# Products of the identity with itself in TensorE's waits, in a kernel of two transformer blocks

## What is computed

```python
a = modulate(rmsnorm(h), shift, scale)
y = conformer_conv(a)     # layer 0: GLU, 31-tap depthwise conv, layernorm, silu, matmul
y = window_attention(a)   # layer 1: 16 heads, 4 kv heads, window 128, plus 256 context keys
h = h + g1 * y
h = h + g2 * conv_ffn(modulate(rmsnorm(h), ...))   # 1024 -> 2*2816, 3-tap conv, silu gate, -> 1024
```

## Time and profile before

| | |
|---|---|
| median of 3 runs | 2484.35 us |
| lowest and highest | 2482.55 and 2489.43 us |
| profiled execution, device time | 2481.34 us |
| profiled execution, span | 2479.5 us |
| mean granted clock over the span | 0.981 |
| TensorE busy | 2360.1 us, 95% |
| VectorE, ScalarE, GpSimd busy | 49%, 35%, 1% |
| moved by DMA | 387.5 MB |

### The profile page before, as it was taken

The page is one execution under the profiler, slowest core; times in us unless marked ns, Lnnn a source line. Parts: engine busy times, 40 slices in busy tenths (PEclk is TensorE's granted clock), DMA queues, the critical chain, the costliest instruction groups (busy, mean ns, idle before and its releaser), DMA issues. The chain is left out here.

```text
span 2479.5 us, 33877 instructions
## 1 busy us (share of the span) xinstructions
PE 2360.1 (95%) x13786; PEld 1808.2 (73%) x13786; DVE 1213.3 (49%) x1866; ACT 860.3 (35%) x1322; POOL 37.1 (1%) x57
## 2 busy tenths in 40 slices
PE   6999999999999999999899999999998889999997
PEld 4994779999999987677688888875897643333322
DVE  3898556552455342674664565754543422233224
ACT  4125553321233242583542344346444310101101
POOL 0000000000000001100000000000000100000000
PEclk8999999999999999999899999999999999999999
DMA  6248612121122142001232232210341669999996
GB/s 247 69 122 306 238 68 71 65 82 46 60 68 73 64 179 69 29 2 68 93 100 96 94 103 93 84 58 2 105 145 45 257 269 409 421 420 422 421 421 268
DMA packets 74242, 387.51 MB, mean 156 GB/s; under 512 B 8576, under 2 KB 12928, under 8 KB 43264
## 3 DMA queue, kind: packets, MB, share of 16 engines
q1 hardware_dynamic: 74112, 385.66, 41.2%
HBM read 380.22 MB, written 2.10 MB: 154 GB/s over the span
## 5 line engine op out<-in xcount | busy, mean ns | idle before, releaser
L314 PE MATMUL PS<-XNH,WHI 128*128 128x384 f32 (+2 forms) x1888 | 593.7, 358 | 16.4 <-issue 4.4
L269 DVE TENSOR_TENSOR WLO<-RAW,WHI 128x1024 fp32r<-128x1024 f32 (+3 forms) x226 | 279.1, 1235 | 645.8 <-ACT WHI L258 645.6
L314 PE MATMUL PS<-XNH,WLO 128*128 128x384 f32 (+2 forms) x1888 | 585.5, 354 | 0.0
L314 PE MATMUL PS<-XNL,WHI 128*128 128x384 f32 (+2 forms) x1888 | 585.1, 353 | 0.0
L258 ACT ACTIVATE WHI<-RAW 128x1024 fp32r<-128x1024 f32 (+3 forms) x226 | 241.5, 1068 | 772.8 <-PE PS L314 755.6
L314 PEld LDWEIGHTS PS<-XNH,WHI 128*128 128x128 f32 x1888 | 348.6, 189 | 52.5 <-issue 17.2
L314 PEld LDWEIGHTS PS<-XNL,WHI 128*128 128x128 f32 x1888 | 349.3, 189 | 32.1 <-issue 3.4
L314 PEld LDWEIGHTS PS<-XNH,WLO 128*128 128x128 f32 x1888 | 349.0, 189 | 29.5
L2994 PE MATMUL PS<-RAWM,XS 128*64 128x512 f32 x1024 | 237.5, 599 | 9.5 <-DMA RAWM<-experts 8.9
L2994 PEld LDWEIGHTS PS<-RAWM,XS 128*64 128x64 f32 x1024 | 68.1, 136 | 140.6 <-issue 104.8
L314 PE MATMUL PS<-HH,WHI 128*128 128x384 f32 (+1 forms) x528 | 158.0, 353 | 0.0
(11 more groups left out here) (358 smaller groups left out, 2560.3 us busy)
## 6 DMA issues: line engine op xcount, KB each, us to landing
RAWM<-experts SPq DMA_DIRECT2D x191, 1024.0 KB, 14.7
RAW<-up SPq DMA_DIRECT2D x88, 512.0 KB, 3.2
ADAW<-ada SPq DMA_DIRECT2D x26, 1024.0 KB, 7.4
RAW<-down SPq DMA_DIRECT2D x32, 704.0 KB, 4.0
ADAG<-ada SPq DMA_DIRECT2D x14, 1024.0 KB, 9.6
RAW<-pw SPq DMA_DIRECT2D x24, 512.0 KB, 3.5
ADAL<-ada SPq DMA_DIRECT2D x8, 1024.0 KB, 7.3
RAW<-qkv SPq DMA_DIRECT2D x12, 512.0 KB, 3.3
```

The costliest lines, as they stand in the source:

```text
L269: dve.tensor_tensor(prog.WLO[:, at % SPLITS, 0:to.length], prog.RAW[:, at % RAWS, 0:to.length], f32(prog.WHI[:, at % SPLITS, 0:to.length]) ...
L314: last = pe.matmul(prog.PS[:, to, at:at + b - a], w, x[:, k, a:b], start=(k == 0 and n == 0), stop=(k == g.k - 1 and n == 2))
```

## The change

A new helper issues n fp32 products of the identity with itself, 128 by 128 by 128, into 128 columns of a PSUM bank. Nothing reads them and no semaphore counts them. 180 of them are placed in TensorE's streams. Two waits are added, both on TensorE: in the attention ahead of the 8 products (both counts are waited for again by the first transposes), and at the end of `project`.

```diff
+def idle_products(prog, pe, bank, n):
+    to = prog.PS[:, bank // 2, bank % 2 * 512:bank % 2 * 512 + P]
+    for _ in range(n):
+        pe.matmul(to, prog.IDENT[:], prog.IDENT[:], start=True, stop=True)
...
 gated_convolution, tensor:
             for n in range(ADA_RING, KD):
                 first.multiply_slice(pe, n)
+            idle_products(prog, pe, 3, 5)
             first.turn_round(pe, 0)
+            idle_products(prog, pe, 3, 9)
...
 LayerNormSilu.on_tensor:
+        idle_products(self.prog, pe, 6, 3)
         pe.wait_ge(self.mean_kept, 1)
         spread_blocks(self.prog, pe, self.mean, ...)
+        idle_products(self.prog, pe, 6, 8)
         for k in range(KD):
+            if k >= 1:
+                idle_products(self.prog, pe, 6, 1)
             pe.wait_ge(self.squared, k + 1)
...
         for n in range(2):
             self.ada.multiply_slice(pe, n)
+        idle_products(self.prog, pe, 6, 5)
         pe.wait_ge(self.inverted, 1)
         spread_blocks(self.prog, pe, self.rstd, ...)
-        for n in range(2, 4):
-            self.ada.multiply_slice(pe, n)
+        self.ada.multiply_slice(pe, 2)
+        idle_products(self.prog, pe, 0, 6)
+        self.ada.multiply_slice(pe, 3)
+        idle_products(self.prog, pe, 0, 5)
...
 convolution_output, tensor:
             for n in range(6, KD):
                 ada.multiply_slice(pe, n)
+            idle_products(prog, pe, 6, 4)
             pe.wait_ge(ada.kept, 1)
...
             multiply_gap_slices(prog, pe, 0, range(GAP_FIRST))
+            idle_products(prog, pe, 2, 4)
...
 project, tensor:
             multiply_all(prog, pe, g, xh, xl, lambda u: segments, psum_free, None)
+            pe.wait_ge(psum_free, 4 + g.n - 3)
+            idle_products(prog, pe, 0, 5)
...
 conv_ffn, tensor (squares is None in ffn1):
             norm.sums_on_tensor(pe)
             if squares is not None:
                 multiply_gap_slices(prog, pe, 0, range(GAP_FIRST, GAP_SLICES))
+            else:
+                idle_products(prog, pe, 3, 6)
             norm.spread_on_tensor(pe)
             if squares is not None:
                 for n in range(GAP_SLICES, KD):
+                    idle_products(prog, pe, 3, 4)
                     ada.multiply_slice(pe, n)
+                idle_products(prog, pe, 3, 6)
+            else:
+                idle_products(prog, pe, 3, 14)
...
 window_qkv, tensor:
             for n in range(GAP_SLICES, KD):
+                idle_products(prog, pe, 3, 6)
                 ada.multiply_slice(pe, n)
...
 window_attention, rest_on_tensor:
         for n in range(1, BUFS):
             scores(pe, n)
+        pe.wait_ge(psum_free, kept(10))
+        pe.wait_ge(sined, 9)
+        idle_products(prog, pe, 5, 8)
         for n in range(STEPS):
...
         values(pe, STEPS - 1)
+        idle_products(prog, pe, 4, 5)
...
 latent_attention, tensor, at the end:
+            idle_products(prog, pe, 0, 7)
...
 memory_output, tensor:
             for n in range(2, len(blocks_of)):
                 turn(n)
+            idle_products(prog, pe, 1, 45)
             pe.wait_ge(slots, 1)
...
             last.then_inc(slot_turned, 1)
+            idle_products(prog, pe, 1, 4)
...
 experts, tensor:
+            idle_products(prog, pe, 1, 4)
             for k in range(KD):
                 gather(0, k)
```

## The result

| | before | after |
|---|---|---|
| median, first comparison (4 and 4 runs) | 2484.14 us | 2469.92 us, ratio 0.9949 [0.9929, 0.9969] |
| median, second comparison (17 and 7 runs) | 2480.84 us | 2469.99 us, ratio 0.9961 [0.9945, 0.9976] |
| profiled execution, device time and span | 2481.34, 2479.5 us | 2470.45, 2468.6 us |
| mean granted clock | 0.981 | 0.992 |
| TensorE busy | 2360.1 us | 2388.0 us |

The change makes the kernel faster by 14.2 us in the first comparison and 10.9 in the second. 2474.0 was forecast, with 2464 to 2482 as the range.

The account below looks back on a forecast made before the run. Experts' DMA bounds the end; ahead of it, blocks follow by barriers and low clock costs where TensorE is late. Terms sum to 9.1 us, 2481.3 to 2472.2; allowing for the higher median gives 2474.0, range 2464 to 2482.

Parts of the forecast that it names:

- The price of a product: All places: one identity product takes 0.24 us of TensorE at full clock and 0.44 at half clock.
- Do the products hold the clock: All places: the added products were expected to keep the clock at 1.00, as a dense run of this shape did.
- rival 2: Products don't hold the clock and run at half; the router's slot turn comes 6.5 us late; 2493.6 us, chance 0.05.
- Gain 2.3: `pw1`: 2.7 us from a full-clock first pair, less a net delay of 0.4; between -1.5 and 3.5.
- nothing is added between the DMA-bound slices: `pw1`: with no products among the slices, the clock falls at 36.29 as before, so five products take 2.2 us.
- ACT's squares are the bound and nothing is won: `pw2`: ACT is busy 3.41 of 3.41 us at 247.9, so no gain; 0.3 us lost over the groups.
- The slice lands at 349.23: `ffn0`: slice 7 and six products end at 351.5, first pair started at 351.66; gain 0.1 us, -0.3 to 1.5.
- a sign of being wrong: `ffn0` and `qkv`: first pairs starting over 0.5 us later than their slice allows would show the prediction wrong.
- The upper bound: `ffn1`: 3.3 us gained if the clock holds at its norm; 1.2 was taken, between -1.5 and 3.3.
- Rival 3: More is held than counted: `ffn1` in full 2.1, `ffn0`'s norm 1.5, low stretches' placement elsewhere 3; 2467 us, chance 0.09.
- Rival 4: Every low microsecond was a loss: TensorE late through all eight stretches, 28 us; 2456 us, chance 0.02.
- Rival 1: Too little is late on TensorE: only `wo`, `mem_in` and the gather gain, 4.6 less 1.2 us; 2481 us, chance 0.24.

Follow-up runs that it names:

- experiment 4: Changed kernel with all 180 products one column wide instead of 128: 2502.68 us, ratio 1.010 to the kernel before.
- experiment 1: Kernel before with only the 20 products at the attention's start and end and the end of `mla`: 2477.9 us against 2480.89, ratio 0.9989.
- experiment 2: Kernel before with only the 107 products in the norms, around the slices and at the end of `project`: 2475.1 us, ratio 0.9981.
- experiment 3: Kernel before with only the 53 products of the router and the gather: 2477.78 us, ratio 0.9990.
- experiment 7: Changed kernel with products also at still-low places, none before `pw1`'s turn round, slightly fewer at `ffn1`'s spread and the slots' wait: 2465.64 us, ratio 0.9935 to before.
- experiment 10: Kernel of experiment 7 without its 34 products inside `pw2`'s layernorm: 2464.49 us, ratio 0.9922 to the kernel before.
- experiment 9: Kernel of experiment 7 with five products ahead of each of `pw1`'s slices 4 to 7: 2464.62 us, ratio 0.9928 to the kernel before.
- experiment 11: Kernel of experiment 9 with two products, not four, ahead of `ffn0`'s slices 6 and 7, and two, not six, behind: 2461.58 us, ratio 0.9922 to before.
- experiment 12: Kernel of experiment 9 once more, unedited, beside experiment 11 on one chip: 2464.44 us, ratio 0.9932 to the kernel before.
- experiment 8: Changed kernel with 90 products instead of 45 in the router's wait for the slots: 2478.76 us, 8.8 above the changed kernel beside it.
- experiment 6: Kernel before once more, no edit: 2476.01 us in its one run.

## Why the prediction was right, and where not

The same TensorE products stand in every profile, so the time between two of their starts can be compared over all. The table has the boundaries by their time in the profile of before, and the mean without and with the change's products at a place (in brackets the number of profiles; experiment 4 left out).

| stretch, us of before | before | after | without | with | gain | forecast |
|---|---|---|---|---|---|---|
| `pw1`, to 242.84 | 242.84 | 242.31 | 242.97 (4) | 242.95 (4) | 0.0 | 2.3 |
| `pw2`, to 268.20 | 25.36 | 25.66 | 26.87 (5) | 25.68 (8) | 1.2 | -0.3 |
| `ffn0`, to 356.27 | 88.07 | 87.60 | 87.37 (4) | 87.99 (8) | -0.6 | 0.1 |
| `qkv`, to 962.33 | 606.06 | 604.50 | 606.46 (4) | 604.78 (4) | 1.7 | -0.1 |
| attention's start, to 1033.58 | 71.25 | 68.88 | 70.82 (4) | 69.11 (9) | 1.7 | 1.8 |
| `wo`'s start, to 1141.41 | 107.83 | 106.23 | 107.42 (4) | 106.22 (9) | 1.2 | 1.5 |
| `ffn1`'s norm, to 1215.39 | 73.98 | 74.66 | 73.54 (4) | 72.78 (4) | 0.8 | 1.2 |
| `mla`'s start, to 1670.38 | 454.99 | 452.12 | 454.24 (4) | 452.51 (4) | 1.7 | none |
| `mem_in`'s start, to 1746.57 | 76.19 | 74.46 | 75.67 (4) | 74.50 (9) | 1.2 | 1.5 |
| router and gather, 1925.09 to 1998.41 | 73.33 | 72.56 | 73.24 (4) | 72.27 (3) | 1.0 | 1.1 |

They add up to 9.9 us, against 10.9 between the medians of the second comparison; 9.1 was forecast. That the sum is so near is in part luck: `pw1` gave 2.3 less than forecast, and `pw2`, `qkv` and `mla` 1.5 to 1.8 more each.

- **The price of a product: right.** 0.225 us at full clock (0.24 taken) and 0.43 at half (0.44 taken). The estimate of 0.32 from the Trainium skill (TensorE: Matmul & The Clock Gate, Back-to-back issue gap) is not borne out: by it the slot turn would be 4.1 us late, and it is 0.05. The row of the same shape was the better source. The slot turn, forecast 0.5 late, came at once.
- **Do the products hold the clock: right**, as experiments 1 to 3 show place by place, but for the attention's, in three of nine profiles. At `wo` and at `mem_in` the clock was full in nine of nine profiles with products and fell in three of four without. In one-column form they don't (experiment 4): rival 2, given 0.05, is a real mechanism that the 128 columns keep away.
- **`pw1`: the step that failed.** "Gain 2.3" was right for the first pair (1.66 ahead in the profile) and wrong for the block. The turn round came 1.92 later, not "1.2 to 1.5", and the first pair 1.01 later where a net delay of 0.4 was forecast: the five products took 2.3 us at half clock. The convolution's slices then waited 0.6 to 2.0 us for their DMA in all five profiles with the five (experiment 4's too), in two of five with others but not these (0.6 each), in none of four with nothing added. I had followed the gain to the end of the pair and not to the end of the block. Without the five (experiments 7 and 10) `pw2` starts 1.0 us sooner than before, and with products between the slices 2.6 to 2.9 (experiments 9, 11 and 12): "nothing is added between the DMA-bound slices" named the right lack. Why the slices' loads come late with the five isn't shown, and a late turn round isn't needed for it. In experiment 8's profile the clock was back before the five, and the turn round started 2.21 us after slice 7, against 2.40 in the first profile of before and 4.16 in that of the changed kernel. It led by 3.8 us at 60 us, but its slices still waited 2.0, and `pw2` started only 1.25 sooner than before:

```profile
36.00 1.06 PE L461 MATMUL PS<-ADAW,SC 128*32 128x512 f32 x8 [1.00 <-DMA ADAW<-ada]
...
38.21 0.96 PE L470 MATMUL PS<-PRM,ADAR 128*128 128x8 f32 x8
```

- **`pw2`: mis-sized.** "ACT's squares are the bound and nothing is won" held for a low stretch of 3.4 us. In four other profiles without products it was 6.8 or 10.2 us long, and in three of them the first pair was slow as well; the mean loss is 1.2 us. The 0.3 forecast as overhang was right against the first profile (25.66 for 25.36).
- **`ffn0`: mis-sized by its cover.** The six products stand between slice 7 and a pair whose XNL is ready at 349.81, and end at 350.95. "The slice lands at 349.23" was true of one execution; in the changed one it starts at 348.60. With the six, the pair starts 2.36 us after slice 7 in all eight profiles. Without products it is 2.43 and 2.07 in the two profiles where the clock fell, and 1.00 in the two where it didn't. So the six cost as much as the fall, 1.4 us more than the slice asks for, which the prediction named as a sign of being wrong. Experiment 11 gets back 0.9 of it.
- **`qkv`** fell at 958 in before and not after, with no product near. Part of its 1.7, like `mla`'s, is that luck.
- **Attention, `wo`, `mem_in`, router: right**, within 0.3 each. The attention's two added waits were never run without the products, so its gain is that of both. In experiment 6 neither `wo` nor `mem_in` fell, which is why the means are 0.3 below the forecast of one profile.
- **`ffn1`: right in its mechanism.** The clock fell as forecast, six products took 2.9 instead of 2.6, the spread came late and the pair ran at full clock. Not foreseen was the fall at 1200.86, behind the 1.82 us wait for WLO; it cost 1.6. The upper bound that the prediction gives, 3.3, is about what its own terms add up to (2.3 + 1.3 - 0.2), and experiment 2's profile gained 3.5. Twelve products at the end of `project` and seven ahead of the third unit win the block for good: 70.4 to 70.5 us in all five profiles that have them.
- **Rival 3** ("the placement of low stretches in other executions") is true in part: 3.4 of the 9.9 lie in `qkv` and `mla`, in each of which the clock fell in three of four profiles of the old stream and in one of four of the new. The Trainium skill (TensorE: Matmul & The Clock Gate, What's actually happening) says that at its start the same kernel measures a different number of slow matmuls from run to run; experiment 6 shows the like at waits in the middle (13.6 us low in `pw2`, not 3.4). What decides where it falls isn't settled here.
- **Rival 4** is refuted: between the two profiled executions 94.8 - 38.9 = 55.9 us of low clock went for 10.9 us, 0.2 each. By the Trainium skill (TensorE: Matmul & The Clock Gate, Terms) it would be a half each; these runs disagree.
- **Rival 1** is refuted by the attention's 1.7, where DVE waited for TensorE, and by experiment 2, faster by 5.8 us without any of the three places that this rival counted.

## What to carry to other kernels

Work that nobody reads pays where TensorE is idle just ahead of a stretch in which it is the bound and the clock would fall. It pays in full only if it ends before the wait does: the 45 products too many were paid in full (10 us), and in front of a hand-over such as `ffn0`'s pair six ate the whole gain. Fill a wait a little short, follow a gain to the end of the block and not of the stretch, and size it from several profiles, since one shows one draw of where the clock falls. One-column products are no cheaper way: here they cost the same time, and the clock fell.

## What the runs showed that was not expected

- A one-column fp32 product takes 0.22 us at full clock, as one of 128 columns does: fewer columns save nothing here.
- TensorE, with products of one column, was busy 13.60 of 13.60 us and stayed at half clock.
- An unfilled wait of 1.99 or 2.74 us ahead of `wo` and `mem_in` brings the clock down in some executions and not in others; the kernel before varied over 18.4 us in 27 runs and over 14.3 in the 11 beside experiment 11, whose kernel, without a low stretch between 30 and 2440 us in its profile, stayed within 1.03 us in 6.
